# Last expert pass of a two-layer mLSTM / Conformer kernel: one ring of seven slots for all loads, in place of two slots for the largest expert and five for the small ones

## The chip, the cores and the metric

One core of a Trainium2 chip runs the whole program. The metric is the device time of one execution in microseconds (us), the median of several runs. TensorE is called PE, its weight loads PEld, VectorE DVE, ScalarE ACT, GpSimd POOL and SyncE SP.

## What is computed

Two layers of a diffusion backbone run for two groups of 128 tokens with width 1024 in float32. Layer 0 is a bidirectional mLSTM mixer and a dense SwiGLU, layer 1 a Conformer convolution mixer and a mixture of eight experts, of which each token takes two. The change lies in the mixture of experts:

```python
def swiglu(t, w1, w2):
    u = t @ w1
    return (jax.nn.silu(u[..., :D_FF]) * u[..., D_FF:]) @ w2

def moe_ffn(h, w_router, w1, w2):          # D_FF = 3584, 8 experts, top 2
    t = h.reshape(B * L, D)
    logits = (t @ w_router).astype(jnp.float32)
    top_v, top_i = lax.top_k(logits, TOP_K)
    probs = jax.nn.softmax(top_v, axis=-1)
    combine = jnp.sum(jax.nn.one_hot(top_i, N_EXPERTS, dtype=jnp.float32) * probs[..., None], axis=1)
    out = jnp.zeros_like(t)
    for e in range(N_EXPERTS):
        out = out + combine[:, e:e + 1].astype(t.dtype) * swiglu(t, w1[e], w2[e])
```

## The kernel before

**The ring.** All weights stream from HBM through `ring`, seven slots of 128 x 3072 float32 (1.573 MB each, 1536 KB). SP issues the loads one after the other, in one queue; `expert_stage(m, row, j)` (L600) is the issue of one expert load into slot j, and the line shown for it is L602. A load may be issued once the slot's former contents have been used. SP waits for that ahead of the issue, so a load that must wait holds all loads behind it.

**Rows and blocks.** An expert's weights are 168 rows of 128 x 512 (`EXPERT_ROWS`); six rows (`PER`) are one load, or stage, so an expert has 28 loads (`FC`), and eight rows (`KD`) are one block, so it has 21 blocks (`BLOCKS`). A load of six rows and a block of eight do not line up: three blocks are four loads.

**The last pass.** The experts are taken by size: expert 0 and the next in ordinary passes, then a pair, and last `big_expert` (L2539), which runs five streams together: the largest expert's weights serve 128 tokens by `expert_row`, with the weights split into a high and a low part (`w_hi` by ACT at L1126, `w_lo` by DVE at L1791, in cuts of three rows), and serve a remainder of 64 tokens, unsplit, by `side_block` (L2381); three small experts, one after the other, run their 63 blocks by `small_block` (L2404). For m = 0 to 20 (this text says block m) PE does `side_block(m)`, the eight rows of the largest expert, a few transposes, and then three blocks of the small experts. Each side block and each small block is 32 matmuls at L2377, each expert row three at L1997 to L1999. For m = 0 the side block comes after the rows. At the end of every side and small block PE adds one to the semaphore `halves_used`; the position of each block in that count is `halves_done(who, b)`. This text calls it **the count**. In the last pass, the side block of m (m >= 1) takes the count to 4m + 21, the three small blocks behind it to 4m + 22, 4m + 23 and 4m + 24; for m = 0 the side block gives 22.

**The order of the loads.** `STREAM` (L219) lists the 112 loads of the pass, 28 of the largest expert ("big", st) and 84 of the small ones (j, st), in the order in which their first block comes. This text numbers them 0 to 111. In the middle of the pass, loads 23 to 32 are (0, 16), (0, 17), (0, 18), big 7, (0, 19), (0, 20), (0, 21), (0, 22), big 8 and big 9. SP issues them in the loop at L637.

**Their slots.** `BIG_IN` gives the largest expert the slots 1 and 2, `SMALL_IN` the small experts the slots 3, 4, 0, 5 and 6. A big load takes the slot of the big load two before it, a small load that of the small load five before it: `in_place_earlier` (L238) names that earlier load and L641 waits for the count of the last block that reads it. For a big load L643 waits as well until DVE has split the earlier one (`split_ready`). The first loads of the pass, without an earlier one, wait for the slots of the pair's pass (L645, L647). The consumers wait on one semaphore per slot, `loaded[...]`, with a number from `place_of`. SP's loop, a dozen lines, stands below with the rest.

Of the kernel before, what the change touches and what calls it, by code (L numbers as in the profile page):

```python
# [23 lines left out]
FC = FF // P  # L24
# [10 lines left out]
SLOTS = 7  # L35
# [178 lines left out]
def halves_done(who, b):  # L214

    return HALVES.index((who, b)) + 1


STREAM = []  # L219
# [1 line left out]
    for _w, _b in [("big", _m)] + small_blocks(_m) + ([(SMALLS - 1, LAST)] if _m == LAST else []):  # L221
        STREAM += [(_w, st) for st in range(_b * KD // PER, (_b * KD + KD - 1) // PER + 1) if (_w, st) not in STREAM]
assert len(STREAM) == (1 + SMALLS) * FC
BIG_IN = (1, 2)
SMALL_IN = (3, 4, 0, 5, 6)
BIG_SLOTS, SMALL_SLOTS = len(BIG_IN), len(SMALL_IN)
assert sorted(BIG_IN + SMALL_IN) == list(range(SLOTS))


def place_of(who, st):  # L230

    if who == "big":
        return BIG_IN[st % BIG_SLOTS], st // BIG_SLOTS
    n = who * FC + st
    return SMALL_IN[n % SMALL_SLOTS], n // SMALL_SLOTS


def in_place_earlier(who, st):  # L238

    n = st - BIG_SLOTS if who == "big" else who * FC + st - SMALL_SLOTS  # L240
    if n < 0:
        return None
    return ("big", n) if who == "big" else (n // FC, n % FC)


PAIR_STREAM = []
# [31 lines left out]
def mlstm_conformer_kernel(nc, vecs, consts, rowc, x_in, pos, w_gate, w_router, mix, ff, moe, c0, norm_out,  # L278
# [7 lines left out]
    with ctx:  # L286
# [42 lines left out]
        def carve(*shape, rows=P):  # L329
            n = int(np.prod(shape))  # L330
            a = work[0:rows, at[0]:at[0] + n]
            at[0] += n
            assert at[0] <= WORK
            if len(shape) == 1:
                return a
            names = "abcd"[:len(shape)]
            return a.rearrange(f"p ({' '.join(names)}) -> p {' '.join(names)}",
                               **{k: v for k, v in zip(names, shape)})
# [80 lines left out]
        has, who = carve(OVER), carve(OVER)  # L419
# [151 lines left out]
        def _(sp):  # L571
# [28 lines left out]
            def expert_stage(m, row, j):  # L600

                sp.dma_start(ring[:, slot(ST_MOE + j), :], moe[bass.ds(row, 1), :, :].rearrange("o p n -> (o p) n")  # L602
                             ).then_inc(loaded[slot(ST_MOE + j)], 16)
# [33 lines left out]
            for w, st in STREAM:  # L637
                k, _ = place_of(w, st)
                earlier = in_place_earlier(w, st)
                if earlier is not None:  # L640
                    sp.wait_ge(halves_used, halves_done(earlier[0], (earlier[1] * PER + PER - 1) // KD))  # L641
                    if w == "big":
                        sp.wait_ge(split_ready, loads * CUTS + (mid_cuts + CUTS + 2 * (earlier[1] + 1)))  # L643
                elif PAIR_END[k][0] == "mid":
                    sp.wait_ge(split_ready, loads * CUTS + (mid_cuts + 2 * (PAIR_END[k][1] + 1)))  # L645
                else:
                    sp.wait_ge(halves_used, halves_done(PAIR, (PAIR_END[k][1] * PER + PER - 1) // KD))  # L647
                expert_stage(None, experts[w] * FC + st, k)
# [102 lines left out]
        def _(act):  # L751
# [365 lines left out]
            def big_high(i, first, end, pair=False):  # L1117

                for s in range(first, end):
                    k, turn = pair_place("mid", s // 2) if pair else place_of("big", s // 2)  # L1120
                    sl = slot(ST_MOE + k)
                    if s % 2 == 0:
                        before = 4 * i + turn if pair else 4 * (i - 1) + PAIR_LOADS[k] + turn
                        act.wait_ge(loaded[sl], before * 16 + 16 * ((ST_MOE + k) // SLOTS + 1))
                    act.wait_ge(stage_used, i * CUTS + (ST_MOE + s - W_BUFS + 1))
                    act.activation(w_hi[:, s % W_BUFS, :], ring[:, sl, s % 2 * CUT * ROW:(s % 2 + 1) * CUT * ROW],  # L1126
                                   ACT.Copy).then_inc(hi_ready, 1)
# [140 lines left out]
        def _(dve):  # L1268
# [517 lines left out]
            def big_low(i, first, end, pair=False):  # L1786

                for s in range(first, end):
                    sl = slot(ST_MOE + (pair_place("mid", s // 2) if pair else place_of("big", s // 2))[0])
                    dve.wait_ge(hi_ready, i * CUTS + (FF_CUTS + s + 1))  # L1790
                    TT(w_lo[:, s % W_BUFS, :], ring[:, sl, s % 2 * CUT * ROW:(s % 2 + 1) * CUT * ROW],  # L1791
                       w_hi[:, s % W_BUFS, :].bitcast(f32), ALU.subtract).then_inc(split_ready, 1)
# [899 lines left out]
```

## Time and profile before

| | us |
|---|---|
| median of 3 runs | 1650.26 (1649.32 to 1651.39) |
| the profiled execution | 1643.76 |
| its span, first to last instruction | 1642.0 |
| its last pass, from the pair's last small block to the last matmul block of a small expert | 1190.3 to 1625.0 |

The profile tells of one execution, which was 6.5 us shorter than the median of the other runs. Times in its views count from the span's start. A page gives, for each engine, its busy time and share, the same in 40 slices (a digit is tenths), the granted clock of PE and the rate of the DMA in each slice. Further views give the idle time of each engine with what ended it (waits), the instructions in order of time (timeline), the sums of a stretch (windows) and the DMA issues with the time from issue to landing.

### The profile page before, as it was taken

The numbers are of one execution on the slowest core, as the hardware profiler recorded it, in microseconds if no ns is written. First come the engines' busy times: TensorE is split into PE (matmuls) and PEld (weight loads), VectorE is DVE, ScalarE is ACT, GpSimd is POOL, SyncE is SP. The second block draws the span as 40 slices with busy tenths as digits, with TensorE's granted clock in tenths as the row PEclk, the third lists the DMA queues.
The fourth block names the chain that finished last, engine by engine and source line by source line (L and its number), as shares of the span: only waits on it lengthen the run. The fifth ranks groups of instructions, "written<-read, shape, count | busy, mean of one in ns | idle before, by whom it ended". The sixth has DMA issues, their size and how long they took to land.

```text
span 1642.0 us, 25250 instructions
## 1 busy us (share of the span) xinstructions
PE 1576.4 (96%) x10116; PEld 1253.1 (76%) x10116; DVE 954.6 (58%) x1339; ACT 682.0 (42%) x846; POOL 56.5 (3%) x105
## 2 busy tenths in 40 slices
PE   5999998899999999999999999999999999999997
PEld 3888885799999877667888887767777777777774
DVE  1777674565555579649999995545533233233353
ACT  2444444543333232337777774534432222222121
POOL 0111110000000000001000000000000000000000
PEclk9999999999999999999999999999999999999999
DMA  9776769635554484349999998999999999999994
GB/s 395 289 265 249 269 244 367 241 116 192 180 178 171 166 344 163 133 169 370 372 381 382 377 377 332 421 424 421 423 415 424 410 401 423 403 404 415 423 426 183
DMA packets 59028, 523.00 MB, mean 319 GB/s; under 512 B 6820, under 2 KB 7716, under 8 KB 14756
## 3 DMA queue, kind: packets, MB, share of 16 engines
q1 hardware_dynamic: 50112, 495.09, 75.7%
q0 software_dynamic: 5392, 19.41, 3.1%
q10 hardware_dynamic: 3412, 6.92, 1.1%
q8 instruction: 81, 1.33, 0.3%
q14 instruction: 31, 0.25, 0.0%
HBM read 503.30 MB, written 18.10 MB: 318 GB/s over the span
## 4 chain that ended last, share of the span: by engine, by line
PE 85%; DMA 6%; DVE 4%; ACT 2%; issue 2%; SPq 0%; DVEq 0%; POOL 0%; ACTq 0%; POOLq 0%
PE ps L2377 20%; PE ps L1997 17%; PE ps L1999 16%; PE ps L1998 16%; DMA ring<-moe 4%; PE ps L2285 3%; DMA ring<-mix 2%; PE ps L1933 2%; PE ps L2165 2%; PE ps L2273 2%; PE ps L2037 1%; DVE w_lo L1791 1%; PE ps L2150 1%; DVE w_lo L1639 1%; PE ps L2459 1%
## 5 line engine op out<-in xcount | busy, mean ns | idle before, releaser
L1791 DVE TENSOR_TENSOR w_lo<-ring,w_hi 128x1536 fp32r<-128x1536 f32 x112 | 192.1, 1755 | 215.8 <-ACT w_hi L1126 215.7
L1126 ACT ACTIVATE w_hi<-ring 128x1536 fp32r<-128x1536 f32 x112 | 161.4, 1481 | 153.0 <-DMA ring<-moe 147.4
L1997 PE MATMUL ps<-w_hi,hg 128*128 128x512 f32 x512 | 205.2, 401 | 5.1 <-DVE hg L1712 2.8
L1639 DVE TENSOR_TENSOR w_lo<-ring,w_hi 128x1536 fp32r<-128x1536 f32 x112 | 193.7, 1755 | 14.3 <-ACT w_hi L1069 14.3
L1998 PE MATMUL ps<-w_lo,hg 128*128 128x512 f32 x512 | 201.0, 393 | 0.0
L1069 ACT ACTIVATE w_hi<-ring 128x1536 fp32r<-128x1536 f32 x112 | 167.1, 1495 | 53.3 <-PE ps L1999 51.3
L1999 PE MATMUL ps<-w_hi,hg 128*128 128x512 f32 x448 | 175.6, 392 | 0.0
L2377 PE MATMUL ps<-ring,xs_a 128*64 128x256 f32 x1344 | 153.7, 381 | 7.4 <-DMA ring<-moe 3.9
L1999 PE MATMUL ps<-w_hi,hid 128*128 128x512 f32 x400 | 156.5, 391 | 0.0
L2377 PEld LDWEIGHTS ps<-ring,xs_a 128*64 128x64 f32 x1344 | 100.8, 137 | 54.5 <-issue 9.7
L1997 PE MATMUL ps<-w_hi,hid 128*128 128x512 f32 x336 | 133.1, 396 | 0.7 <-DVE hid L1766 0.7
L1997 PE MATMUL ps<-hg,w_hi 128*128 128x256 f32 x448 | 128.0, 286 | 3.5 <-issue 3.5
L1998 PE MATMUL ps<-w_lo,hid 128*128 128x512 f32 x336 | 131.3, 391 | 0.0
L2377 PE MATMUL ps<-ring,xn 128*64 128x256 f32 x1120 | 125.2, 380 | 5.0 <-ACT so L1149 5.0
L1545 DVE TENSOR_TENSOR w_lo<-ring,w_hi 128x1536 fp32r<-128x1536 f32 x56 | 96.1, 1754 | 58.5 <-ACT w_hi L989 58.5
L1999 PE MATMUL ps<-hg,w_lo 128*128 128x256 f32 x448 | 127.9, 285 | 0.0
L1997 PEld LDWEIGHTS ps<-w_hi,hg 128*128 128x128 f32 x512 | 96.9, 189 | 35.1 <-issue 11.6
L2377 PEld LDWEIGHTS ps<-ring,xn 128*64 128x64 f32 x1120 | 89.4, 137 | 36.2 <-issue 7.3
L1998 PEld LDWEIGHTS ps<-w_lo,hg 128*128 128x128 f32 x512 | 97.0, 189 | 19.0
L989 ACT ACTIVATE w_hi<-ring 128x1536 fp32r<-128x1536 f32 x56 | 80.4, 1481 | 68.7 <-PE ps L1999 68.7
L2377 PE MATMUL ps<-ring,so 128*64 128x256 f32 x896 | 102.3, 380 | 1.1 <-ACT so L1149 1.1
L1999 PEld LDWEIGHTS ps<-w_hi,hg 128*128 128x128 f32 x448 | 84.4, 188 | 18.0
(344 smaller groups left out, 2579.6 us busy)
## 6 DMA issues: line engine op xcount, KB each, us to landing
ring<-moe SPq DMA_DIRECT2D x224, 1536.0 KB, 11.1
ring<-mix SPq DMA_DIRECT2D x92, 1024.0 KB, 6.6
ring<-ff SPq DMA_DIRECT2D x28, 1536.0 KB, 6.4
xg<-work POOLq DMA_DIRECT2D x11, 512.0 KB, 6.0
yg<-work POOLq DMA_DIRECT2D x8, 512.0 KB, 4.4
so<-xg POOLq DMA_DIRECT2D x6, 512.0 KB, 9.0
work<-c POOLq DMA_DIRECT2D x8, 257.0 KB, 4.6
c_out<-work ACTq DMA_DIRECT2D x8, 257.0 KB, 5.9
```

Of the source, the lines that this page charges most:

```text
L989: act.activation(w_hi[:, (2 * c + j) % W_BUFS, :], ring[:, slot(n), j * CUT * ROW:(j + 1) * CUT * ROW], ACT.Copy).then_inc(hi_ready, 1)
L1069: act.activation(w_hi[:, s % W_BUFS, :], ring[:, sl, s % 2 * CUT * ROW:(s % 2 + 1) * CUT * ROW], ACT.Copy).then_inc(hi_ready, 1)
L1126: act.activation(w_hi[:, s % W_BUFS, :], ring[:, sl, s % 2 * CUT * ROW:(s % 2 + 1) * CUT * ROW], ACT.Copy).then_inc(hi_ready, 1)
L1545: TT(w_lo[:, n % W_BUFS, :], ring[:, slot(ST_FF + c), j * CUT * ROW:(j + 1) * CUT * ROW], w_hi[:, n % W_BUFS, :].bitcast(f32), ALU.subtrac ...
L1639: TT(w_lo[:, s % W_BUFS, :], ring[:, slot(ST_MOE + s // 2), s % 2 * CUT * ROW:(s % 2 + 1) * CUT * ROW], w_hi[:, s % W_BUFS, :].bitcast(f32 ...
L1791: TT(w_lo[:, s % W_BUFS, :], ring[:, sl, s % 2 * CUT * ROW:(s % 2 + 1) * CUT * ROW], w_hi[:, s % W_BUFS, :].bitcast(f32), ALU.subtract).th ...
L1933: ins = pe.matmul(ps[32 * j:32 * j + 32, MODB, :], silu_c[:, k, :], w[:, j * ADA_COLS:(j + 1) * ADA_COLS], start=(k == 0), stop=(k == KD - 1))
L1997: pe.matmul(out, a_hi, b_hi, start=start, stop=False)
L1998: pe.matmul(out, a_hi, b_lo, start=False, stop=False)
L1999: return pe.matmul(out, a_lo, b_hi, start=False, stop=stop)
L2285: ins = pe.matmul(ps[:, UB + s % 2, j * T:(j + 1) * T], w[:, (j * KD + k) * P:(j * KD + k + 1) * P], hT[:, k, :], start=(k == 0), stop=(k ...
L2377: ins = pe.matmul(ps[h * SIDE:(h + 1) * SIDE, bank, col * n:(col + 1) * n], tokens_64, w[:, h * n:(h + 1) * n], start=start, stop=stop)
```

## The change

`place_of` and `in_place_earlier` no longer look at whose load it is. Load n of `STREAM` goes into slot `COME_FREE[n % 7]`, and waits for load n - 7 to have been used. The first seven take the slots in the order in which the pair's pass frees them. The order of the loads, all that PE, ACT, DVE and POOL do, and the kernel's other passes stay as they are; the slots that the last pass reads and the numbers of its waits follow from the two functions.

```diff
-BIG_IN = (1, 2)
-SMALL_IN = (3, 4, 0, 5, 6)
-BIG_SLOTS, SMALL_SLOTS = len(BIG_IN), len(SMALL_IN)
-assert sorted(BIG_IN + SMALL_IN) == list(range(SLOTS))
+COME_FREE = (1, 3, 4, 2, 0, 5, 6)
+assert sorted(COME_FREE) == list(range(SLOTS))
 
 
 def place_of(who, st):
 
-    if who == "big":
-        return BIG_IN[st % BIG_SLOTS], st // BIG_SLOTS
-    n = who * FC + st
-    return SMALL_IN[n % SMALL_SLOTS], n // SMALL_SLOTS
+    n = STREAM.index((who, st))
+    return COME_FREE[n % SLOTS], n // SLOTS
 
 
 def in_place_earlier(who, st):
 
-    n = st - BIG_SLOTS if who == "big" else who * FC + st - SMALL_SLOTS
-    if n < 0:
-        return None
-    return ("big", n) if who == "big" else (n // FC, n % FC)
+    n = STREAM.index((who, st)) - SLOTS
+    return STREAM[n] if n >= 0 else None
...
                 if earlier is not None:
                     sp.wait_ge(halves_used, halves_done(earlier[0], (earlier[1] * PER + PER - 1) // KD))
-                    if w == "big":
+                    if earlier[0] == "big":
                         sp.wait_ge(split_ready, loads * CUTS + (mid_cuts + CUTS + 2 * (earlier[1] + 1)))
```

Worked out from these functions, in the steady state, whose pattern repeats every three blocks and sixteen loads, SP waits for these counts. A count at which a load waits holds for those behind it too:

| load | 21 | 22 | 23 | 24 | 25 | 26 | 27 | 28 | 29 | 30 | 31 | 32 | 33 | 34 | 35 | 36 |
|---|---|---|---|---|---|---|---|---|---|---|---|---|---|---|---|---|
| count before | 33 | 34 | 34 | 35 | 36 | 37 | 38 | 38 | 39 | 40 | 41 | 41 | 42 | 42 | 43 | 44 |
| count after | 34 | 34 | 37 | 37 | 37 | 37 | 38 | 41 | 41 | 41 | 41 | 42 | 42 | 42 | 43 | 44 |

The counts 37 and 41 are the side blocks of m = 4 and m = 5.

On SP's queue in the middle of the pass, this stands for the loads 28 to 31 before (`L602` is the issue, `L643` belongs to a load whose predecessor must also have been split):

```order
L602 ISA [waits halves_used]
L602 DMA ring<-moe 128x3072
L602 ISA [waits halves_used]
L602 DMA ring<-moe 128x3072
L602 ISA [waits halves_used]
L602 DMA ring<-moe 128x3072
L643 REGISTER_ALU [waits halves_used]
L602 ISA [waits split_ready]
L602 DMA ring<-moe 128x3072
```

and this after, where the lines stand six higher:

```order
L637 REGISTER_ALU [waits halves_used]
L596 ISA [waits split_ready]
L596 DMA ring<-moe 128x3072
L596 ISA [waits halves_used]
L596 DMA ring<-moe 128x3072
L596 ISA [waits halves_used]
L596 DMA ring<-moe 128x3072
L596 ISA [waits halves_used]
L596 DMA ring<-moe 128x3072
```

The wait for a slot of the largest expert has moved from load 31, the largest expert's own, to load 28, a small expert's, with three loads behind it.

At the start of the pass, this stands for the loads 4 to 6 before (`L645` belongs to a slot that the pair's pass frees):

```order
L645 REGISTER_ALU
L602 ISA [waits split_ready]
L602 DMA ring<-moe 128x3072
L643 REGISTER_ALU [waits halves_used]
L602 ISA [waits split_ready]
L602 DMA ring<-moe 128x3072
L602 ISA [waits halves_used]
L602 DMA ring<-moe 128x3072
```

and this for the loads 4 to 7 after:

```order
L639 REGISTER_ALU
L596 ISA [waits split_ready]
L596 DMA ring<-moe 128x3072
L596 ISA [waits halves_used]
L596 DMA ring<-moe 128x3072
L596 ISA [waits halves_used]
L596 DMA ring<-moe 128x3072
L637 REGISTER_ALU [waits halves_used]
L596 ISA [waits split_ready]
L596 DMA ring<-moe 128x3072
```

The first wait for a load of the pass itself has moved from load 5 to load 7.

## Rows read from the trace of the kernel before

**Rows 1.** The page: busy us, share, instructions; then clock and rate in 40 slices.

```profile
PE 1576.4 (96%) x10116; PEld 1253.1 (76%) x10116; DVE 954.6 (58%) x1339; ACT 682.0 (42%) x846; POOL 56.5 (3%) x105
...
PEclk9999999999999999999999999999999999999999
...
GB/s 395 289 265 249 269 244 367 241 116 192 180 178 171 166 344 163 133 169 370 372 381 382 377 377 332 421 424 421 423 415 424 410 401 423 403 404 415 423 426 183
```

**Rows 2.** Windows: two stretches of 62 us, about three blocks each, in the last pass.

```profile
core 0: us, PE busy (x) PEld busy (x) DVE busy (x) ACT busy (x) POOL busy (x), PEclk, DMA share, GB/s
1242.00:1304.00 62.00, 60.60 (x474) 45.94 (x472) 18.97 (x19) 15.14 (x18) 0.00 (x0) 1.00 0.99 415
1304.00:1366.00 62.00, 60.60 (x474) 45.92 (x472) 19.05 (x19) 15.74 (x19) 0.00 (x0) 1.00 0.98 409
```

**Rows 3.** Waits from 1175 us to the end: who for whom, us, times, longest.

```profile
ACT w_hi L1126 <- DMA ring<-moe: 142.5, 28, 9.6
...
PE ps L2377 <- ACT so L1149: 8.7, 13, 0.8
...
PEld ps L2377 <- DMA ring<-moe: 0.5, 1, 0.5
```

**Rows 4.** Timeline of PE in blocks 4 to 6: start us, us, instruction, idle before.

```profile
1269.99 3.65 PE L2377 MATMUL ps<-ring,xn 128*64 128x256 f32 x32
...
1290.53 3.62 PE L2377 MATMUL ps<-ring,xs_a 128*64 128x256 f32 x32
1294.09 0.50 PE L1997 MATMUL ps<-w_hi,hg 128*128 128x512 f32 x1
...
1300.62 7.13 PE L2377 MATMUL ps<-ring,xs_a 128*64 128x256 f32 x64 [0.56 <-ACT so L1149]
...
1311.01 3.65 PE L2377 MATMUL ps<-ring,xs_a 128*64 128x256 f32 x32
```

**Rows 5.** Timeline of SP: issues of loads 26, 27, 30, 31, 59 and 62.

```profile
1273.88 0.33 SPq L602 DMA_DIRECT2D ring<-moe  x1
...
1283.98 0.33 SPq L602 DMA_DIRECT2D ring<-moe  x1
...
1290.89 0.33 SPq L602 DMA_DIRECT2D ring<-moe  x1
...
1294.41 0.33 SPq L602 DMA_DIRECT2D ring<-moe  x1
...
1407.55 0.33 SPq L602 DMA_DIRECT2D ring<-moe  x1
...
1414.46 0.33 SPq L602 DMA_DIRECT2D ring<-moe  x1
```

**Rows 6.** DMA issues 27, 30, 59, 62, each alone: count, size, us to landing.

```profile
ring<-moe SPq DMA_DIRECT2D x1, 1536.0 KB, 6.5
...
ring<-moe SPq DMA_DIRECT2D x1, 1536.0 KB, 11.1
...
ring<-moe SPq DMA_DIRECT2D x1, 1536.0 KB, 8.6
...
ring<-moe SPq DMA_DIRECT2D x1, 1536.0 KB, 12.7
```

**Rows 7.** Timeline of SP at the pass's start: issues of loads 4 and 5.

```profile
1183.17 0.33 SPq L602 DMA_DIRECT2D ring<-moe  x1
...
1200.77 0.33 SPq L602 DMA_DIRECT2D ring<-moe  x1
```

**Rows 8.** Windows around two waits of PE, and its timeline behind the first.

```profile
740.00:750.00 10.00, 7.47 (x26) 5.98 (x27) 9.35 (x42) 5.61 (x5) 4.71 (x4) 0.83 0.76 273
1066.00:1076.00 10.00, 8.63 (x54) 5.85 (x53) 2.71 (x2) 1.18 (x1) 0.00 (x0) 1.00 0.99 418
...
742.53 0.50 PE L1997 MATMUL ps<-w_hi,hg 128*128 128x512 f32 x1 [2.82 <-DVE hg L1712]
```

## The prediction

> **What bounds the kernel now.** I read the page first: PE is busy 96% of the span, at full clock, and from slice 26 to slice 39, which hold the pair's pass and the last one, the DMA moves 401 to 426 GB/s, where no slice before them has more than 395 [rows 1]. So two resources are near their end at once, and the question is which of them leads. The windows say it [rows 2]: in 62 us, three blocks, PE is busy 60.6 us at clock 1.00, and the DMA share is 0.98 to 0.99. The waits say who waits for whom [rows 3]: PE stands 8.7 us in the whole pass for ACT's copy of a transposed block (L1149, a round trip of at most 0.8 us), and its weight load 0.5 us, once, for a transfer. ACT, though, waits 142.5 us for loads of the largest expert: these land only just in time, and PE is covered by the little that is left. **PE bounds the pass, and the ring keeps just ahead of it.**
>
> The timeline gives PE's beat [rows 4]: side block of m = 4 at 1269.99, of m = 5 at 1290.53, of m = 6 at 1311.01, so a block is 20.5 us. A side block takes 1294.09 - 1290.53 = 3.56 us, 0.445 us for each of its eight rows. The rate of a full queue is 426 GB/s [rows 1], so one load of 1.573 MB takes 3.69 us, and three blocks need 16 loads, 59.0 us of 61.6. The DMA may stand still for 2.6 us in three blocks and no more; and how late a single load lands counts too.
>
> **The change part by part.** It adds no instruction to PE, ACT, DVE or POOL and moves none; only what SP waits for changes, and with it when each load is issued. SP's queue is in order, so what matters is the highest count waited for up to each load, the table of the section on the change.
>
> *The first loads.* Before, load 5 is a big one and waits for the first one's slot: SP issues load 4 at 1183.17 and load 5 at 1200.77 [rows 7], and loads 6 and 7 stand behind it. After, loads 5 and 6 take slots that the pair's last block frees at 1190.3, 10 us earlier. PE does not wait for them before [rows 3], so this is worth nothing on the path, and at most the 0.5 us that its weight load waits once.
>
> *Loads 28 to 31.* Before, they are issued one by one, at the counts 38, 39, 40 and 41. After, load 28 waits for a slot that the largest expert holds until the side block of m = 5 is over, and 29 to 31 stand behind it: all four go out together at that point, 1294.41 in the time of the trace [rows 5], where load 31 alone goes today. By then the queue has run dry (load 27 was issued at 1283.98 and landed after 6.5 us, [rows 5, 6], or a few us later behind four others), so nothing is in flight. Who needs them: load 31 is big 8, whose first row is the first of the side block of m = 6, at 1311.01. Load 32, big 9, released at the next count but fifth in the queue anyway, is needed at that block's seventh row, 1311.01 + 6 x 0.445 = 1313.7. From the issue, the fifth load of the burst has 1313.7 - 1294.4 = 19.3 us.
>
> What a burst takes, the rows show where the queue was nearly empty before. Load 27 lands after 6.5 us, and load 30, the fourth from it, at 1290.89 + 11.1 = 1302.0, 18.0 us after the first's issue [rows 5, 6]. Load 59 takes 8.6 us and load 62 lands at 1414.46 + 12.7 = 1427.2, 19.6 us after the first's [rows 5, 6]. The fifth follows 3.69 us later: 21.7 and 23.3 us. So PE waits **2.4 to 4.0 us**, partly ahead of the side block of m = 6 and partly in it.
>
> *Loads 23 to 26.* The same happens one block earlier: before, they go out at the counts 34, 35, 36 and 37, after, all at 37, which is 1273.88 [rows 5]. Load 26 is big 7, needed at the third row of the side block of m = 5, 1290.53 + 2 x 0.445 = 1291.4, 17.5 us later. The fourth of a burst lands after 18.0 to 19.6 us. PE waits **0.5 to 2.1 us** more. Load 27 is released at 38 in both and is hidden as today. The third block of the three has no burst at all: loads 33 to 36 wait for the counts 42 to 44 in both.
>
> *What comes behind a wait.* ACT (L1126) and DVE (L1791) make `w_hi` and `w_lo` of the late load while PE does the rest of the side block (3.56 us), as they already do today when ACT waits for the landing; so I add nothing for the split. The issues that follow move with PE, and the DMA has then stood still for as long as PE, so no lag is made up. The waits add to the time one for one.
>
> **The sum.** Both bursts recur every three blocks, the five-load one at m = 3, 6, 9, 12, 15 and 18, the other at m = 5, 8, ... 20: six times each. At the quick end (4th after 18.0 us) a period costs 2.4 + 0.5 = 2.9 us, at the slow end 4.0 + 2.1 = 6.1 us, so 17.4 to 36.6 us in all. The quick end is the undisturbed queue; load 59 has other transfers beside it. I take the quick end for most and the slow end for one or two of six, 17.4 + 1.5 x 3.2 = 22.2, **22 us**. Against the profiled execution that is 1643.8 + 22 = 1666; I keep its distance to the median and forecast 1650.3 + 22 = **1672 us**.
>
> What speaks for the change is its plain logic, that seven slots in one round let each load go as soon as a slot is free. That holds if slots come free in the order in which they were filled. A big slot does not: its last reader is the side block of the next m, so it is held past the small blocks whose slots were filled after it, and today only big loads wait for it.
>
> **The rivals.**
>
> *Quicker bursts.* If loads issued together into an empty queue follow each other at the bare rate, the fifth lands 6.5 + 4 x 3.69 = 21.3 us after the issue and the fourth after 17.6: 2.0 + 0.1 us, 13 us in all, and with 0.5 us less for the first landing 9 us: 1659 to 1663. For it: the first loads of a burst have no older traffic in front. Against: load 30 came after 18.0, not 17.6 [rows 5, 6]. 0.14.
>
> *Hidden after all.* The fifth load would have to land within 19.3 us, 2.4 us before the quickest that the rows show. Then 1650 to 1655. A formula comes near it: the Trainium skill, "DMA: Bandwidth & Descriptors", section "Anatomy of one DMA", puts a transfer at about 2.0 us plus its bytes at 436 GB/s (it was fitted to DMAs issued from GpSimd, and these are SP's); by it, as an estimate, the fifth lands after 2.0 + 5 x 3.61 = 20.0 us, which makes 0.7 us a period and 4 us in all, 1654. The rows are nearer to 21.7, since a single load takes 6.5 us here [rows 6] where the formula has 5.6. 0.08.
>
> *Faster.* The other runs are 6.5 us longer than the profiled one. Should that be late loads in the last pass, then the 10 us that loads 5 and 6 gain at its start would return up to 6.5 us: 1644. It decides if PE's waits for loads are longer in those runs than the new bursts cost. Against it: the profiled run has one such wait, of 0.5 us [rows 3], and the head start is used up at the first burst, two blocks later. 0.04.
>
> *The clock gives way.* Behind a wait of 2.82 us (its matmul at 742.53) the granted clock is 0.83 over 10 us, some 3.4 us at 1.2 GHz, which costs 1.7 us; with the waits of PE near 1069, where it is idle 1.4 us of 10 in all, the clock stays at 1.00 [rows 8]. Here the 2.4 us come in two pieces with side rows between them. If the clock fell at the five-load burst each time, that would be 6 x 1.7 = 10 us, 1682, which is inside the forecast's range; with both bursts at the slow end it is beyond, 1690 and more. The Trainium skill, "TensorE: Matmul & The Clock Gate", section "HAM oscillation", says that waits for a DMA between short groups of matmuls can drop the clock at every tile; of the rows, the one at 742.53 agrees with it and the one near 1069 does not. 0.06 for beyond 1687.
>
> That the change does not do what it says is out: the order shows the waits moved as described.
>
> **How the numbers follow.** The forecast, bursts that cost 17 to 37 us, has 0.68: 1667 to 1687. Quicker bursts 0.14, hidden 0.08, faster 0.04, beyond 1687 0.06. The range leaves out the hidden and the faster case and what is beyond: 1659 to 1687, with 0.82. A measurement of this kernel can tell about 0.2%, 3.3 us, from no change; half of the hidden case is above that. Faster 0.04, within 0.2% 0.04, slower 0.92.
>
> **What the profile after would show.** PE (or its weight load) waits for ring loads at L2377, some 12 to 18 times, 17 us or more in total, in two of every three blocks; side blocks of m = 6, 9, 12 ... that are 1 us longer, with a wait ahead; SP issues four loads within 2 us at the end of a side block, and the issue to landing of the fourth near 17 us; a last pass longer by the same 22 us, with all before 1190 unchanged; a DMA rate in it of about 400 instead of 415 GB/s. I am wrong if PE shows no such waits, or if they are there but the beat of 20.5 us stays, which would mean that they replace the wait for ACT; wrong in size if the fourth load of a burst lands well before or after 18 us.

## The result and the profile after

| | median us | runs | against before |
|---|---|---|---|
| before | 1650.8 | 4 | |
| after | 1680.5 (1677.8 to 1684.2) | 4 | 1.0188 (1.0172 to 1.0204) |

The change makes the kernel 29.7 us slower. The profiled execution of after took 1684.17 us, 3.7 us more than the median; its span is 1682.4.

The page of after, in the lines that answer [rows 1]:

```profile
PE 1590.8 (95%) x10116; PEld 1253.8 (75%) x10116; DVE 953.9 (57%) x1339; ACT 681.5 (41%) x846; POOL 56.4 (3%) x105
...
PEclk8899999999999999999999999999999999999999
...
GB/s 397 241 260 258 274 240 360 234 115 186 188 188 163 216 278 195 80 230 398 373 380 379 373 361 371 426 423 426 420 357 385 394 358 398 397 352 409 383 379 189
```

PE's share falls by one point only, which by itself would tell little. The rate tells more: the slices of the last pass, which had 401 to 426 GB/s, now have 352 to 409. The windows of after confirm it, about three blocks each, with the columns of [rows 2]:

```profile
1249.00:1315.00 66.00, 61.75 (x476) 45.08 (x473) 18.88 (x19) 15.04 (x18) 0.00 (x0) 1.00 0.93 385
1315.00:1382.00 67.00, 61.59 (x474) 45.20 (x472) 18.96 (x19) 15.64 (x19) 0.00 (x0) 1.00 0.92 378
```

The same 474 to 476 matmuls take 66 to 67 us where they took 62, at the full clock, and the DMA share is 0.92 to 0.93 where it was 0.98 to 0.99. The waits of after from 1175 us to the end, beside [rows 3]:

```profile
ACT w_hi L1120 <- DMA ring<-moe: 232.7, 28, 14.7
...
PEld ps L2371 <- DMA ring<-moe: 38.9, 31, 4.4
...
PE ps L2371 <- DMA ring<-moe: 26.2, 24, 4.0
PE ps L2371 <- ACT so L1143: 8.7, 13, 0.8
```

PE's wait for ring loads, absent before, is new: 24 times, 26.2 us. The wait for ACT's copy is 8.7 us as before; the new waits come on top of it.

How one such wait looks stands in the timeline of PE around block 6, to be laid beside [rows 4]:

```profile
1311.72 7.13 PE L2371 MATMUL ps<-ring,xs_a 128*64 128x256 f32 x64 [0.57 <-ACT so L1143]
1318.64 3.65 PE L2371 MATMUL ps<-ring,so 128*64 128x256 f32 x32
1324.22 2.81 PE L2371 MATMUL ps<-ring,xs_a 128*64 128x256 f32 x24 [1.92 <-DMA ring<-moe]
1327.91 1.08 PE L2371 MATMUL ps<-ring,xs_a 128*64 128x256 f32 x8 [0.88 <-DMA ring<-moe]
```

The side block of m = 6, one piece of 32 matmuls before, starts after an idle time of 1.92 us and is cut after its sixth row, 24 matmuls, where PE is idle again for 0.88 us. SP's timeline from 1305 to 1308 us shows the cause, four issues in 2 us at the end of the side block of m = 5:

```profile
1305.50 1.99 SPq L596 DMA_DIRECT2D ring<-moe  x4
```

and the DMA issues of the first of these four, of the fourth, issued at 1307.08, and of load 32, issued at 1315.56, give their time to landing:

```profile
ring<-moe SPq DMA_DIRECT2D x1, 1536.0 KB, 6.3
...
ring<-moe SPq DMA_DIRECT2D x1, 1536.0 KB, 17.1
...
ring<-moe SPq DMA_DIRECT2D x1, 1536.0 KB, 12.3
```

Load 31 lands at 1324.2, the moment at which PE's side block starts; load 32 lands at 1327.9, the moment at which its last eight matmuls start.

**Where the time sits, block by block.** From PE's timelines of both kernels I took the time from the end of one side block to the end of the next. After minus before, in us:

| block m | 3 | 6 | 9 | 12 | 15 | 18 | sum |
|---|---|---|---|---|---|---|---|
| behind the burst of loads 28 to 31 | 3.5 | 3.3 | 2.8 | 3.0 | 3.6 | 5.8 | 22.0 |

| block m | 5 | 8 | 11 | 14 | 17 | 20 | sum |
|---|---|---|---|---|---|---|---|
| behind the burst of loads 23 to 26 | 0.2 | 1.7 | 1.1 | 1.5 | 2.2 | 1.5 | 8.2 |

Block 19 adds 0.9 and the end of the pass 1.9. The other blocks (4, 7, 10, 13, 16) differ by less than 0.05 us. Together these are 33.0 us, and the last pass as a whole went from 434.7 to 467.7 us. The waits read as 26.2 us, less than the 33.0. The end of a matmul is modelled: a block of 32 is shown as 3.65 us, but the next one starts 3.46 us later (1307.55 and 1311.01 in the trace of before). So an idle time is shown about 0.2 us too short, 24 times, and once the clock fell, which cost 1.4 us (below); together that makes 32.4.

The medians grew by 29.7 us, the pass of the profiled execution by 33.0. There is one traced execution of each kernel, and the traced one of after was above its median; whether the pass was shorter in the others is not known.

### The profile page after: what moved, and what is told of

Same layout as the page of the kernel before. It is cut to its first block, busy times and chain, and to the rows that moved or that the text cites. A ratio compares the mean times of both kernels' runs of the same rounds, so it can differ in the third digit from the quotient of the medians.

```text
span 1682.4 us, 25252 instructions
## 1 busy us (share of the span) xinstructions
PE 1590.8 (95%) x10116; PEld 1253.8 (75%) x10116; DVE 953.9 (57%) x1339; ACT 681.5 (41%) x846; POOL 56.4 (3%) x105
## 4 chain that ended last, share of the span: by engine, by line
PE 73%; DMA 17%; DVE 5%; ACT 2%; issue 2%; SPq 1%; DVEq 0%; POOL 0%; ACTq 0%; POOLq 0%
PE ps L1991 16%; PE ps L1993 15%; PE ps L1992 15%; DMA ring<-moe 15%; PE ps L2371 12%; PE ps L2279 3%; DMA ring<-mix 3%; PE ps L2159 2%; PE ps L2267 1%; PE ps L1927 1%; PE ps L2031 1%; DVE w_lo L1785 1%; DVE w_lo L1633 1%; PE ps L2144 1%; SPq L596 1%
## 5 line engine op out<-in xcount | busy, mean ns | idle before, releaser
L2371 PE MATMUL ps<-ring,xs_a 128*64 128x256 f32 x1344 | 157.3, 385 | 28.4 <-DMA ring<-moe 25.0
L2371 PEld LDWEIGHTS ps<-ring,xs_a 128*64 128x64 f32 x1344 | 97.4, 138 | 83.8 <-DMA ring<-moe 36.1
L1991 PEld LDWEIGHTS ps<-w_hi,hg 128*128 128x128 f32 x512 | 96.8, 189 | 34.5 <-issue 12.8
L1992 PEld LDWEIGHTS ps<-w_lo,hg 128*128 128x128 f32 x512 | 96.9, 189 | 18.9
L1991 PE MATMUL ps<-ring_r 128*128 128x256 f32 x336 | 98.0, 292 | 0.0
```

Of the source, the lines that this page charges most:

```text
L1991: pe.matmul(out, a_hi, b_hi, start=start, stop=False)
L1992: pe.matmul(out, a_hi, b_lo, start=False, stop=False)
L2371: ins = pe.matmul(ps[h * SIDE:(h + 1) * SIDE, bank, col * n:(col + 1) * n], tokens_64, w[:, h * n:(h + 1) * n], start=start, stop=stop)
```

## The experiments

All ran beside the kernel before. For each I give the length of its last pass too, from the pair's last small block to the last small block of the pass, read from its PE timeline. It is the sharper number, since the part ahead of it varies from run to run for a reason of its own, shown further down.

| kernel | median us | ratio to before (95%) | last pass us | PE waits for loads in it, us |
|---|---|---|---|---|
| before | 1648.9 to 1650.8 in three groups | | 434.7 | 0 |
| after | 1680.5 | 1.0188 (1.0172 to 1.0204) | 467.7 | 26.2 |
| waits_alone | 1681.0 | 1.0188 (1.0168 to 1.0207) | 467.8 | 24.0 |
| burst_five | 1671.7 | 1.0140 (1.0122 to 1.0158) | 456.7 | 18.7 |
| burst_four | 1659.6 | 1.0071 (1.0051 to 1.0090) | 445.1 | 7.9 |
| first_free | 1650.0 | 1.0002 (0.9992 to 1.0012) | 434.5 | 0 |
| half_after | 1647.8 | 0.9992 (0.9979 to 1.0005) | 434.4 | 0 |
| half_before | 1648.8 | 0.9998 (0.9987 to 1.0010) | 434.5 | 0 |
| five_earlier | 1652.7 | 1.0035 (1.0019 to 1.0050) | 439.9 | 2.9 |
| five_later | 1737.7 | 1.0542 (1.0524 to 1.0561) | 527.5 | 66.3 |

### The waits without the slots

```diff
+HELD = {}
+for _n in range(SLOTS, len(STREAM)):
+    _w, _s = STREAM[_n - SLOTS]
+    HELD[_n] = max(halves_done(_w, (_s * PER + PER - 1) // KD), HELD.get(_n - 1, 0))
+HOLD = {_n: _c for _n, _c in HELD.items() if _n % 16 in (0, 1, 2, 3, 4, 5, 6, 7, 8, 9, 10, 11, 12, 13, 14, 15)}
...
-            for w, st in STREAM:
+            for n, (w, st) in enumerate(STREAM):
                 k, _ = place_of(w, st)
+                if n in HOLD:
+                    sp.wait_ge(halves_used, HOLD[n])
```

> The kernel before, with its own slots (two for the largest expert, five for the small ones), and only the changed kernel's waits added: from load 7 on, SP also waits for the count that the changed kernel waits for. Loads 5 and 6 keep the late issue of before. Theory (loads held back at the side blocks, then landing in a burst): the whole loss comes with the waits, so 27 to 30 us over before, 1678 to 1681, with PE idle for ring loads some 24 to 27 us in the last pass; the changed kernel's early issue of loads 5 and 6 is worth at most 1 us. Rival (where the data lie, or the numbers waited for on each slot's semaphore, costs the time): within 3 us of before, 1651.

Measured 1681.0 us, 31.9 over before (a little above the 27 to 30 expected), and a pass of 467.8 us, the changed kernel's to 0.1 us. That close a match is in part luck, since single blocks differ both ways (block 6 grew by 4.0 us here and by 3.3 in after, block 19 by 0.5 and 0.9). The slots themselves, and the numbers on their semaphores, cost nothing that can be read; **the loss is in the waits**. The early issue of loads 5 and 6, which this kernel lacks, is worth nothing that can be read.

### Each burst by itself

The same edit, with `_n % 16 in (12, 13, 14, 0)`:

> The kernel before, with the extra waits for the loads 12 to 14 and 16 of every sixteen alone (28, 29 and 30 wait for count 41, 32 for 42; the same at every third block). Theory: the waits of PE at the side blocks of m = 3, 6, ... 18 remain, which sum to 17.8 us in the changed kernel's trace, so 16 to 21 us over before, 1667 to 1672. Rival (what counts is the idle DMA, which must be made up somewhere, so either burst alone is covered by the 2.6 us of spare DMA time in three blocks): 0 to 5 us.

and with `_n % 16 in (7, 8, 9)`:

> The kernel before, with the extra waits for the loads 7 to 9 of every sixteen alone (23, 24 and 25 wait for count 37). Theory: the waits of PE at m = 5, 8, ... 20, some 6 us in the changed kernel's trace, so 5 to 9 us over before, 1656 to 1660. If the two bursts are independent, this and the other one add up to the changed kernel's 30 us. Rival (spare DMA time covers it): 0 to 2 us.

The waits of PE for loads, of burst_five and then of burst_four:

```profile
PE ps L2386 <- DMA ring<-moe: 18.7, 16, 3.5
...
PE ps L2386 <- DMA ring<-moe: 7.9, 11, 2.0
```

The passes are 22.0 and 10.4 us longer than before's, 32.4 together, against 33.1 for all waits. So each burst costs time by itself, and the totals nearly add up. Place by place they do not: of the 10.4 us of burst_four only 6.8 lie at the blocks 5, 8, ... 20, and 3.7 at the blocks 6, 9 and 18, which the other burst hits too. At block 18 the two alone cost 2.6 and 5.4 us, and all waits together 5.4. Counted from the before measured beside them, both medians came out above what I expected (+22.7 for 16 to 21, +10.5 for 5 to 9). For burst_five the reason is that I had taken the sum from the waits as the trace shows them, which are too short; for burst_four it is the loss at the three blocks that I had not counted. The rival, that 2.6 us of spare DMA time in three blocks would cover either, falls: the spare time exists but is not where the late load needs it.

### Half the bytes

In the last pass each load brings only the first 1536 columns of its slot. The other half is old data, so the last experts are computed with wrong weights; all instructions and waits stay.

```diff
-                expert_stage(None, experts[w] * FC + st, k)
+                sp.dma_start(ring[:, slot(ST_MOE + k), 0:STAGE // 2],
+                             moe[bass.ds(experts[w] * FC + st, 1), :, 0:STAGE // 2].rearrange("o p n -> (o p) n")
+                             ).then_inc(loaded[slot(ST_MOE + k)], 16)
```

> The changed kernel, in whose last pass each load brings only the first half of its slot (128 x 1536, 0.786 MB); the other half is left as it was, so the output is not the reference's. All waits, counts and slots are the changed kernel's. Theory (a burst's four loads go out in time, but are moved too slowly one behind the other, 3.7 us each): with half the bytes the fourth and fifth land some 7 us earlier, more than the 2 to 4 us that they are late, so PE's waits for ring loads in the last pass vanish and the time is before's, 1648 to 1652. Rival (SP's late issue alone, or the clock, or the slots, costs the time): 1670 or more.

> The kernel before with the same halved loads in its last pass. Theory (PE bounds the pass, no load is late): within 2 us of before, 1649 to 1652. This is the floor of anything that the placing of loads can give. Rival (late loads cost something in the runs, the last pass is bound in part by the DMA): 3 to 7 us less, 1644 to 1648.

The waits of ACT for loads and of PE for ACT, of half_after and then of half_before:

```profile
ACT w_hi L1122 <- DMA ring<-moe: 104.0, 25, 8.6
...
PE ps L2373 <- ACT so L1145: 8.7, 13, 0.8
...
ACT w_hi L1128 <- DMA ring<-moe: 9.1, 3, 5.3
PE ps L2379 <- ACT so L1151: 8.7, 13, 0.8
```

With the changed kernel's waits, slots and issue times but half the bytes, the whole loss is gone: 434.4 us of pass. ACT still waits 104.0 us for loads of the largest expert, and that costs nothing now, since PE is covered. And before with half the bytes is 434.5 us too, though ACT hardly waits for a load any more. So **434.5 us is the pass's length without any late load (the 8.7 us of PE's waits for ACT's copies are in it), and the kernel before already stood on it**: no way of placing loads can make its 434.7 shorter by more than 0.3 us. These 0.3 us lie in block 18, where its weight load waited once for a load [rows 3]. This is also why ACT's 142.5 us of waiting in [rows 3] were no loss, only the sign of how little cover was left.

### The release one small block sooner, and one count later

burst_five's edit once more, with `_n % 16 in (12, 13, 14)` and `_c - 1` (loads 28 to 30 held until 40), then with `_n % 16 in (12, 13, 14, 15)` and `_c + 1` (28 to 31 until 42). Neither holds load 32 by itself, as burst_five does:

> The kernel before, with the loads 12 to 14 of every sixteen (28, 29, 30) held until the count 40, one small block (3.5 us) sooner than in the changed kernel; load 31 waits for 41 as before. Theory: the fourth and fifth landings come 3.5 us earlier than where they were 2.4 to 4 us late, so nearly all of the loss goes: 0 to 4 us over before. Rival (a burst of loads costs by itself, whenever it is released, through the DMA or the queue): 10 us or more over before.

> The kernel before, with the loads 12 to 15 of every sixteen (28 to 31) held until the count 42, about 10 us later than in the changed kernel. Theory: PE waits for load 28 itself, needed right behind the count 42, for the 6.5 us that one load takes, and then for the ones behind it: the fifth now is 10 us later still, so 12 to 15 us in each of six periods, 75 to 92 us over before, 1726 to 1743. Rival (waits are mostly made up by what PE finds ready afterwards): under 50 us.

Measured +3.8 and +88.8 us in medians, passes of +5.2 and +92.8 us. Together with burst_five (+22.0 at the count 41) this is the dose. 3.5 us sooner takes 17 of the 22 us away. One count later adds 70.8. That count comes 10.1 us after the other (in after, load 28 goes out at 1305.50 and load 32, which waits for 42, at 1315.56), and the release is late seven times, at the six blocks and once more at the end of the pass (loads 108 to 111): 7 times 10.1 is 70.7, and the seven places grew by 9.0 to 12.0 us each over burst_five, the slower clock (below) included. Past the point at which the cover is used up, each us of delay costs a us of PE's time, and before it, nothing or nearly nothing. Of the 5.2 us left at 40, 3.9 lie in the blocks 18 and 19, behind the longest wait, where the clock fell as well: single matmuls of the largest expert's rows are shown as 0.63 us there, as 0.39 elsewhere.

```profile
1568.13 1.10 PE L2386 MATMUL ps<-ring,xs_a 128*64 128x256 f32 x8 [2.34 <-DMA ring<-moe]
```

The waits in five_later are long enough to show something more, in PE's timeline:

```profile
1320.06 3.67 PE L2386 MATMUL ps<-ring,xs_a 128*64 128x256 f32 x32 [0.57 <-ACT so L1158]
1330.28 6.10 PE L2386 MATMUL ps<-ring,xs_a 128*64 128x256 f32 x32 [6.55 <-DMA ring<-moe]
1336.22 3.62 PE L2386 MATMUL ps<-ring,so 128*64 128x256 f32 x32
1342.89 2.40 PE L2386 MATMUL ps<-ring,xs_a 128*64 128x256 f32 x10 [3.05 <-DMA ring<-moe]
```

Thirty-two matmuls take 6.10 us behind the wait of 6.55 us, and 3.62 in the next block. The windows of five_later, with the columns of [rows 2], give the clock:

```profile
1310.00:1323.00 13.00, 12.43 (x88) 9.25 (x86) 3.28 (x4) 1.10 (x3) 0.00 (x0) 1.00 0.01 5
1323.00:1336.00 13.00, 6.45 (x38) 3.57 (x36) 0.00 (x0) 0.00 (x0) 0.00 (x0) 0.74 0.86 343
```

The first line shows the held release itself: 13 us with a DMA share of 0.01. The second shows a granted clock of 0.74, so about half of the stretch is at 1.2 GHz. The block behind such a wait takes 2.5 us more. Not all of that reaches the end: at 1342.89 PE waits again, 3.05 us, for a later load of the same burst, and with quicker matmuls in between that wait would have been longer. What the clock costs in the whole pass was not separated.

### A ring that takes the slot which comes free first

```diff
-    n = STREAM.index((who, st))
-    return COME_FREE[n % SLOTS], n // SLOTS
+def plan_slots():
+    used = [halves_done(w, (st * PER + PER - 1) // KD) for w, st in STREAM]
+    place, earlier, holds = [], [], {}
+    for n in range(len(STREAM)):
+        k = COME_FREE[n] if n < SLOTS else min(holds, key=lambda s: (used[holds[s][0]], holds[s][0]))
+        before, turn = holds.get(k, (None, -1))
+        holds[k] = (n, turn + 1)
+        place.append((k, turn + 1))
+        earlier.append(before)
+    return place, earlier
```

> Each load takes the slot whose contents are used first, by the count at which they are done, whoever owns it. In the steady state this gives the very counts of before; only loads 5 and 6 (and load 111, by one) go out earlier, as in the changed kernel. Theory (no load of the last pass is late before, so a head start is worth nothing): within 1.5 us of before, 1649 to 1652, with the last pass still 434 to 435 us long. Rival (the head start gives back what late landings cost in the runs that are longer than the profiled one): 3 to 6.5 us faster, 1644 to 1648.

The waits of PE in its last pass:

```profile
PE ps L2386 <- ACT so L1158: 8.7, 13, 0.8
PEld ps L2386 <- DMA ring<-moe: 0.3, 1, 0.3
```

Measured 1650.0 us, 1.0002 of before (0.9992 to 1.0012), a pass of 434.5 us. Loads 5 and 6 go out at 1196.6, as the pass begins, as in the changed kernel, and it gains nothing. This is the ring that the change meant: it never issues a load later than either the divided ring or the changed one. That it equals before fits the counts: from load 7 to load 110 the division in 2 and 5 slots waits for the very same ones.

## Why the prediction was right, and where it was off

The forecast was 1672 us, the range 1659 to 1687; measured were 1680.5. The mechanism and its places were right, and the size was put too low by a quarter to a third: 22 us forecast, 29.7 measured in medians and 33.0 in the traced pass. By its steps:

- **What bounds the pass.** PE, with the ring just ahead: right. Half the bytes leave the pass at 434.5 us.
- **The first loads worth nothing.** Right (first_free, waits_alone).
- **Loads 28 to 31 go out together at the end of the side block of m = 5, and PE waits ahead of the side block of m = 6 and in it, at its seventh row.** Right to the place, [rows 4] against the timeline of after, and in the six places named. The size was given as 2.4 to 4.0 us: it is 2.8 to 3.6 in five and 5.8 in the sixth.
- **Nothing in flight at the burst.** Not quite: in after, load 27 was issued at 1294.87 and landed after 11.7 us, at 1306.6, 1.1 us behind the first issue of the burst. The engines had little left to move, a DMA share of 0.06:

```profile
1305.00:1306.00 1.00, 1.00 (x8) 0.69 (x5) 1.00 (x2) 0.62 (x2) 0.00 (x0) 1.00 0.06 25
```

  So the first load took 6.3 us, as if alone.
- **Loads 23 to 26, one block earlier, 0.5 to 2.1 us.** Right: 0.2 to 2.2 us, mean 1.4.
- **Nothing for the split.** Right: the waits of after have none of PE at the largest expert's rows, neither for ACT nor for DVE.
- **Waits add one for one, nothing is made up.** Right: the blocks in between are the same to 0.05 us.
- **The sum, the step that was off.** I took the quick end for most of the periods, because load 30 in [rows 5, 6] seemed the undisturbed case and load 59 the disturbed one, with "other transfers beside it". The trace of before shows none of size: from 1405 to 1417 us all queues but SP's moved 0.02 MB, one packet. In after, the fifth load of a burst landed 22.0 to 22.7 us after the first's issue in five of the six and 25.2 in one, against 21.7 and 23.3 at my two ends. Five of the six lie between the ends; the choice between them was wrong. The middle, 3.2 + 1.3 = 4.5 us a period and 27 in all, would have given 1677. So what I had taken for a disturbance is the usual case: in most bursts one load or another lands up to 1.6 us later than 3.7 us behind the one ahead of it. What delays it is open. The kernel before has such delays too (load 59 itself, 8.6 us where load 27 took 6.5) and no wait of PE behind them.
- **The burst beyond the slow end**, at block 18 (5.8 us). Here the trace does show other transfers. POOL issues two gathers while the burst is under way, and from 1583 to 1596 us their queue (`q0`) moves 1.05 MB beside the loads:

```profile
1579.31 0.94 POOL L738 DMA_INDIRECT so<-yg,dest  x1 [33.78 <-DVE x L1826]
1580.55 0.94 POOL L738 DMA_INDIRECT so<-yg,dest  x1 [0.30 <-issue]
...
q1 hardware_dynamic: 390, 4.23, 78.5%
q0 software_dynamic: 288, 1.05, 22.0%
```

  At 426 GB/s, 1.05 MB are 2.5 us by my estimate, and the fifth load was 2.4 to 3.2 us later than in the other five. All kernels issue these gathers; that they are the cause is read from the time at which they run, no experiment left them out.
- **Left out of the sum:** load 21's kind (held at 34 instead of 33), harmless except at block 19, where PE waits 0.70 us for such a load (101) and the block grew by 0.9 us; a seventh burst, loads 108 to 111 at the last side block, 1.9 us at the end. Both stand in the pattern of the table that I had, and I only summed its two obvious rows.
- **Quicker bursts.** Out: the fourth loads came after 17.6 to 20.7 us, 18.9 in the mean, only one of the twelve at the 17.6 of that rival, and nothing of the loss was missing.
- **Hidden after all, with the formula of the Trainium skill ("DMA: Bandwidth & Descriptors", "Anatomy of one DMA").** Out: in the burst of loads 28 to 32 the first load took 6.3 us where the formula has 5.6, and the fifth landed after 22.4 where it has 20.0, as an estimate. The measurement decides: with these 1.573 MB loads from SP the formula is too quick by 0.7 us for one and 2.4 us for five in a row.
- **Faster, by what the other runs are longer than the profiled one.** Out, and the place of that difference turned up. Most of it lies in the first 100 us. The windows of 0 to 100 us, of before and then of first_free, have a granted clock of 0.98 and 0.90:

```profile
0.00:100.00 100.00, 78.36 (x488) 61.11 (x488) 48.10 (x107) 37.11 (x68) 12.79 (x32) 0.98 0.83 328
...
0.00:100.00 100.00, 78.34 (x436) 59.62 (x436) 43.61 (x99) 33.99 (x62) 11.42 (x29) 0.90 0.79 307
```

  SP's 23rd DMA goes out at 74 us in the first and 6.6 us later in the second, and this difference is 6.6 us still at 256 us and 6.1 at 1162. In all nine other traces that DMA goes out 3.7 to 6.6 us later, and PE was at 1.2 GHz for 14 to 24 of the first 100 us, against 3.4 us in the profiled run of before. That the clock causes the difference is likely but not shown by an experiment. The last pass begins at 1190.3 in the profiled run of before and at 1194.0 to 1197.7 in all nine others, though nothing ahead of it was changed. So of the list of signs, that all before 1190 would stand as it was did not hold.
- **The clock gives way.** It did once in the changed kernel, behind the longest wait, in block 18:

```profile
1584.96 3.65 PE L2371 MATMUL ps<-ring,so 128*64 128x256 f32 x32
1592.57 4.24 PE L2371 MATMUL ps<-ring,xs_a 128*64 128x256 f32 x24 [3.96 <-DMA ring<-moe]
```

  Twenty-four matmuls take 4.24 us instead of 2.81, so 1.4 us. At the other five bursts of this run the clock stayed at 1.00. The length of the wait alone does not decide. In waits_alone the clock fell twice, behind waits of 2.13 and 3.44 us; in burst_five PE waited 2.10 and 3.50 us at the same two side blocks (6 and 18), and the clock stayed. Here is the shorter one of waits_alone, whose first 30 matmuls take 5.14 us, where 30 take about 3.4:

```profile
1322.06 5.14 PE L2386 MATMUL ps<-ring,xs_a 128*64 128x256 f32 x30 [2.13 <-DMA ring<-moe]
```

  The Trainium skill, "TensorE: Matmul & The Clock Gate", section "HAM oscillation", has a clock that falls anew at every wait for a DMA between short groups of matmuls. five_later agrees, where it fell at each of the seven waits of over 6 us; in the changed kernel, whose waits are shorter, it fell at one burst of six.

Of the signs that I named, the number of waits was too low (24 against 12 to 18), and the rate of the DMA too high (378 and 385 GB/s in the two windows against about 400); the landing of the burst's fourth load, near 17 us from its own issue, was 17.1 in the burst shown.

## What to carry to other kernels

A ring that hands slots out in the order of filling is only as good as the order in which they are emptied. Where one stream holds its slots longer, and the issuing queue is in order, its slot stands in the way of loads that belong to others; write down, for each load, the highest count waited for up to it, before and after, and compare these two rows: the places of all losses here stand in them, though not their size. Then give each late release a deadline (who reads the load, and when) and a landing time taken from the same position in a burst, not from a single transfer; the idle share of an engine or of the DMA says nothing about it. And if halving the bytes leaves the time as it is, stop working on the placement of loads.

## What was not expected of the hardware

A burst of loads of 1.573 MB into a queue that had run dry, or nearly, gave landings at 6.3, 10.5, 14.2, 18.7 and 22.4 us from the first issue (loads 28 to 32): the spacing is the 3.7 us of the rate, or up to 0.8 us more, but the first load takes 2.6 us above it, and so did the first of most other bursts (6.3 to 6.7 us in ten of twelve, 7.4 and 8.6 in the two ahead of the side blocks 11 and 17). A divided wait of PE, 1.9 and 0.9 us with 24 matmuls between, left the clock at its full level, as did four more like it; single waits of 2.1 and 3.4 us (waits_alone), 2.3 us (five_earlier) and 4.0 us (after) and all of over 6 us were followed by a stretch at 1.2 GHz, while one of 3.5 us (burst_five) was not. And the same instructions ahead of the last pass took 3.7 to 7.4 us longer in nine executions than in one; most of that arises in the first 100 us, where the granted clock also differs (0.90 against 0.98 in the two compared). The length of the pass, read from the timeline, repeated to 0.3 us (434.4 to 434.7 in four kernels).
